# A hybrid encoder step on one core: scores from stacked float32r halves, attention groups in the order B, C, B, C, A, C, A, A

## The chip, the cores and the metric

The kernel runs on one core of a Trainium2 chip. The metric is the device time in microseconds of one execution; lower is less time. Engines are named TensorE (PE in the rows; PEld is its weight load), VectorE (DVE), ScalarE (ACT), GpSimd (POOL) and SyncE (SP), which issues all transfers of this kernel.

## The reference

Two layers are applied to a prompt of 1024 tokens and to 8 samples of 16 new tokens with 256 past tokens each (1152 token rows in all, in 9 tiles of 128; tile 8 is the samples). Everything is float32. For each layer:

```
h = rms_norm(x, norm_mix);  qa,ka,va,qb,kb,vb,qc,kc,vc,fz = split(h @ w_in)      # q and k of each head normed
A: 6 q heads, 2 k/v heads, 64 wide: softmax(q k/8 + bias, window of own and 2 previous chunks of 64, a sink in the sum) v
B: 4 heads, two maps of 32: softmax(q0 k0 ..) - lam * softmax(q1 k1 ..), times v, then a norm    # bias, all earlier chunks
C: 6 heads, 64 wide: softmax(q k/8 + cum_q - cum_k, causal) v                     # cum: running sum of log forget gates
x = x + concat(A, B, C) @ w_out
x = x + (silu(h2 @ w_gate) * (h2 @ w_up)) @ w_down,  h2 = rms_norm(x, norm_ffn)
```

The caches of keys, values and gates are outputs too.

## The kernel before, in words

`build` runs `setup` once and then, in a loop over the layers, `project`, `attend`, `mix` and `feed`. Each of them is a phase: it has its own buffers and semaphores, and the engines meet at its end. x stays in SBUF for the whole run.

`setup` (lines 149 to 232) loads x, turns the bias table into rows of 10 heads (stored at L180), and loads them back skewed: tiles with 16 rows outermost (L187, L188), and the samples' pieces with 8 batches outermost (L193, L194).

`project` computes h @ w_in in 6 blocks of columns times 9 tiles. Each product is three passes of float32r (high x high, high x low, low x high: L410 to L412); `split_hi` (ScalarE, L238) and `split_lo` (VectorE, L243) make the halves. Raw weights pass through a ring of 4. VectorE reads the result out into `nat`, norms the heads, SyncE stores it to the scratch tensor `qkv` and to the caches (L539), TensorE transposes q and k back to back with later units, ScalarE takes them out into `tT` (a ring of 4), and SyncE stores them as float32 to the scratch `qkT` (1792 rows of 1152 tokens, L512).

`attend` goes through 8 groups, each of two heads (four maps in B), in the order written at line 806: A, A, A, B, B, C, C, C. A group has 18 units: 2 heads times 9 tiles of 128 queries. Each engine runs the same loop over iterations u in program order. TensorE: `score(u)` (plain float32 products of q with the keys, 128 to 1024 columns in pieces of 512, L988; the samples at L995 and L997), `turn(u - 2)` (transposes of p, L1013), extra transposes of past keys (L1027) or of finished outputs (L1035), `values(u - 3)` (L1050, L1059). VectorE: `front(u)` adds the bias row and takes the maximum in one instruction (L1175), then makes the bias of the exponential (L1179 to L1186); `back(u - 1)` makes the reciprocal and, in B, combines the two maps (L1204); `take_out` scales the output, one instruction a unit (L1225). ScalarE: the exponential with its row sum (L1091), the copies of the transposed p (L1105). In A and C, q of a head lies in the upper or lower 64 of 128 partitions with zeros elsewhere (GpSimd clears them, L958, L964), so one product with all 128 rows of kT gives one head; B does so with 32 rows.

SyncE's program sets when a group's data come. `load_front(g)` waits until group g - 2 has been scored (two buffers), loads kT (L888), the bias or gate rows (L891 to L901) and qT (L904) on one semaphore, which `score` waits for at the group's first unit, then v (L907). `load_past(g)` loads past keys (L920), past values (L927), which wait until all values of group g - 1 are multiplied, and the samples' queries `qpast` (L935), which wait for GpSimd's clear (L962) after group g - 1's last score. The order is

```
load_front(groups[0]); ...constants...; load_past(groups[0]); load_front(groups[1])
for g in groups:
    load_past(groups[g.index + 1])
    load_front(groups[g.index + 2])
    sp.wait_ge(evacuated, place["mix", g.index, 2] + 1); sp.dma_start(t["mixT"]..., mixTb[:])     # L952
```

`mix` multiplies the stored outputs by w_out in three float32r passes and adds to x (L1334); `feed` is the FFN (L1526 adds to x), with loops over 22 blocks of D_FF, and stores y (L1408).

Of the kernel before, what the change touches and what calls it, by code (L numbers as in the profile page):

```python
# [19 lines left out]
P = 128  # L20
D_MODEL, SEQ, DEPTH, DEC_BATCH, DEC_SEQ, PAST = 1024, 1024, 2, 8, 16, 256
CHUNK, HEAD = 64, 64
# [4 lines left out]
EPS, NEG = 1e-6, -1e30  # L27
TP = SEQ // P
T = TP + 1
# [15 lines left out]
GAINS = [("q_norm_a", 0, 6, HEAD, HEAD ** -0.5), ("k_norm_a", 384, 2, HEAD, None),  # L45
         ("q_norm_b", 512, 8, B_DIM, B_DIM ** -0.5), ("k_norm_b", 768, 8, B_DIM, None),
         ("q_norm_c", 1024, 6, HEAD, HEAD ** -0.5), ("k_norm_c", 1408, 6, HEAD, None)]
GAIN_AT = [0, 512, 768, 1024, 1408]

# [12 lines left out]
def constants():  # L62
# [16 lines left out]
        "c_causal": np.where(i[None, :] <= i[:, None], 0.0, NEG).astype(np.float32),  # L79
        "c_batch": np.where(same, 0.0, NEG).astype(np.float32),  # L80
        "c_batch_causal": np.where(same & (i[None, :] <= i[:, None]), 0.0, NEG).astype(np.float32),
# [20 lines left out]
class Phase:  # L102
# [16 lines left out]
    def close(self):  # L119
        with self.nc.Block() as block:  # L120
            @block.gpsimd
            def _(pool):
                numbers = sorted(s.num for s in self.sems)
                assert numbers == list(range(numbers[0], numbers[-1] + 1))
                pool.sem_clear(range(numbers[0], numbers[-1] + 1))
        self.ctx.close()
# [6 lines left out]

def build(nc, t):

    with ExitStack() as ctx:
        def sb(name, shape, dt=F32):
            return ctx.enter_context(nc.sbuf_tensor(name, shape, dt))

        k = {"x": sb("x", [P, T, D_MODEL]), "ident": sb("ident", [P, P]),  # L140
             "ms": sb("ms", [P, T]), "logf": sb("logf", [P, T, C_HEADS]), "cumq": sb("cumq", [P, T, C_HEADS]),
             "lam": sb("lam", [P, 1])}
        setup(nc, t, k)
        with nc.Fori(0, DEPTH) as layer:
            project(nc, t, k, layer)
            attend(nc, t, k, layer)
            mix(nc, t, k, layer)
            feed(nc, t, k, layer)


def setup(nc, t, k):
# [19 lines left out]
    with nc.Block() as block:  # L171
# [46 lines left out]
        def _(dve):  # L218
            dve.wait_ge(loaded, 48)
            dve.wait_ge(product, 1)  # L220
            dve.tensor_copy(row[:], pr[:, 0:REL]).then_inc(copied, 1)
            dve.wait_ge(tiles_in, 16 * (2 * P // COPIES + 2 * heads))

            dve.memset(tile_a[0:64, :, 192:256], NEG).then_inc(tiles_done, 1)
            dve.memset(tile_a[64:128, :, 0:64], NEG).then_inc(tiles_done, 1)
            dve.memset(tile_b[0:64, :, SEQ - 64:SEQ], NEG).then_inc(tiles_done, 1)
# [73 lines left out]
class GateSums:  # L300
# [7 lines left out]
    def __init__(self, nc, ph, t, k, layer, xn, h32, pt):  # L308
# [18 lines left out]
        self.lam_s, self.lam_e = rows_[:, at:at + 2], rows_[:, at + 2:at + 4]  # L327
        self.prow, self.srow = pt[:, 0, :], pt[:, 1, 0:PAST]
        self.cols, self.nrow = pt[:, 1, 512:512 + T * C_HEADS], pt[:, 1, PAST:PAST + P]
        self.loaded, self.past_sum, self.col_sums, self.totals, self.sums, self.negated, self.stored = (  # L330
            ph.sem(n) for n in ("gate_loaded", "past_sum", "col_sums", "totals", "sums", "negated", "cum_stored"))
# [3 lines left out]
    def load(self, sp):  # L335
# [10 lines left out]
        sp.dma_start(self.lam_c, t["c_lam"][0:1, bass.ds(layer, 1)].broadcast_to([P, 1])).then_inc(self.loaded, 16)  # L346

    def store(self, sp):
        sp.wait_ge(self.negated, 3)
# [32 lines left out]
    def dve_totals(self, dve):  # L382

        dve.wait_ge(self.past_sum, 1)
        dve.tensor_scalar(self.past_row, self.srow[0:self.BH, :], -1.0, None, ALU.mult).then_inc(self.negated, 1)
        dve.tensor_scalar(self.total, self.is_batch, self.srow[0:self.BH, PAST - 1:PAST], None, ALU.mult).then_inc(self.totals, 1)
        dve.wait_ge(self.col_sums, 1)
        dve.tensor_copy(self.k["cumq"][:, 0:TP, :], self.cols[:, 0:TP * C_HEADS].rearrange("p (t h) -> p t h", t=TP)).then_inc(self.totals, 1)

    def pe_totals(self, pe):  # L390

        new, cols = self.k["logf"][:, TP, :], self.cols[:, TP * C_HEADS:T * C_HEADS]
# [1222 lines left out]
```

## Time and profile before

| | us |
|---|---|
| median of 3 runs | 3482.25 (3479.91 to 3482.97) |
| profiled execution, its own time | 3486.92 |
| its span, first to last instruction | 3485.3 |
| TensorE busy | 3209.2 (92%) |
| weight loads busy | 2875.4 (83%) |
| VectorE busy | 1688.8 (48%) |
| ScalarE busy | 1076.2 (31%) |
| GpSimd busy | 354.5 (10%) |
| DMA: moved, mean share of 16 engines | 274.95 MB, 28% |

Layer 1 runs: setup and start to 78 us, projection to 408, attention to 828, output projection to 941, FFN to 1769; layer 2 repeats it, with its attention from 2108 to 2528. A share is busy time over the stretch; "granted clock" is the part of TensorE's full 2.4 GHz that it was given. The DMA share is the mean over 16 engines, so one engine busy alone shows as 0.06. Every DMA in this kernel goes through SyncE's queue, and an entry of that queue's timeline is the time to issue, not to move.

### The profile page before, as it was taken

Reading aid. Unit: us, or ns where it says so; the run is one execution under the profiler, and the core shown is the slowest. Engines: PE = TensorE matmul, PEld = TensorE weight load, DVE = VectorE, ACT = ScalarE, POOL = GpSimd, SP = SyncE. Lnnn points to the kernel's source line nnn. Section 1 sums busy time; section 2 is a strip of 40 time slices with the busy share of each in tenths; the row PEclk is TensorE's granted clock in tenths of the full one; section 3 lists DMA queues with packets and bytes.
Section 4 is the critical chain, followed back from the end, with each engine's and each line's share of the span. In section 5 each row is a group of like instructions: output and inputs, shape, how many; then the busy total and the mean of one; then the engine's idle time right before and its main releaser. Section 6 shows DMA issues by size and latency. Waiting matters only on the chain. (4 is left out here: it accounts for less than half of the span.)

```text
span 3485.3 us, 50528 instructions
## 1 busy us (share of the span) xinstructions
PE 3209.2 (92%) x18146; PEld 2875.4 (83%) x18146; DVE 1688.8 (48%) x4058; ACT 1076.2 (31%) x2321; POOL 354.5 (10%) x216
## 2 busy tenths in 40 slices
PE   0699899998899999999968997999988999999999
PEld 0589777786799999999957896777778999999998
DVE  0344378644245445445445445784433454454454
ACT  1332266554231111111123225665524111111112
POOL 0222010000010100100012211010001001001000
PEclk9899899998999999999989998999999999999999
DMA  7244554333021111111024445525132111111111
GB/s 175 79 138 137 158 122 107 88 83 117 19 67 37 54 36 36 54 36 36 24 90 127 135 137 139 132 70 131 35 103 67 37 36 54 36 38 52 36 36 61
DMA packets 368395, 274.95 MB, mean 79 GB/s; under 512 B 128546, under 2 KB 336366, under 8 KB 368186
## 3 DMA queue, kind: packets, MB, share of 16 engines
q1 hardware_dynamic: 368218, 272.70, 28.0%
q8 instruction: 98, 1.61, 0.2%
q14 instruction: 79, 0.65, 0.1%
HBM read 195.84 MB, written 78.62 MB: 79 GB/s over the span
## 5 line engine op out<-in xcount | busy, mean ns | idle before, releaser
L1526 DVE TENSOR_TENSOR x<-x,ffn_down 128x512 f32<-128x512 f32 x792 | 509.5, 684 | 0.0
L1548 DVE TENSOR_TENSOR ffn_xn<-ffn_xn,ffn_up 128x384 f32<-128x384 f32 x132 | 73.2, 554 | 752.7 <-ACT ffn_xn L1493 752.7
L410 PE MATMUL ffn_up<-ffn_h_hi,ffn_hi_g 128*128 128x384 f32 x1056 | 355.4, 337 | 2.0 <-DVE ffn_h_lo L243 2.0
L410 PE MATMUL ffn_up<-ffn_h_hi,ffn_hi_u 128*128 128x384 f32 x1056 | 355.2, 336 | 0.0
L412 PE MATMUL ffn_up<-ffn_h_hi,ffn_lo_g 128*128 128x384 f32 x1056 | 354.8, 336 | 0.0
L412 PE MATMUL ffn_up<-ffn_h_hi,ffn_lo_u 128*128 128x384 f32 x1056 | 354.8, 336 | 0.0
L411 PE MATMUL ffn_up<-ffn_h_lo,ffn_hi_g 128*128 128x384 f32 x1056 | 354.8, 336 | 0.0
L411 PE MATMUL ffn_up<-ffn_h_lo,ffn_hi_u 128*128 128x384 f32 x1056 | 354.8, 336 | 0.0
L988 PE MATMUL att_S<-att_kT,att_qT 128*128 128x512 f32 (+3 forms) x864 | 324.1, 491 | 32.7 <-DMA att_qT<-scratch_qkT 25.7
L1493 ACT ACTIVATE ffn_xn<-ffn_up 128x384 f32<-128x384 f32 x132 | 64.9, 492 | 858.5 <-PE ffn_up L412 858.5
L410 PE MATMUL prj_acc<-prj_w_hi,prj_h_hi 128*128 128x384 f32 (+2 forms) x864 | 318.1, 368 | 0.0
L411 PE MATMUL prj_acc<-prj_w_lo,prj_h_hi 128*128 128x384 f32 (+2 forms) x864 | 309.3, 358 | 0.0
L412 PE MATMUL prj_acc<-prj_w_hi,prj_h_lo 128*128 128x384 f32 (+2 forms) x864 | 309.0, 358 | 0.0
L410 PE MATMUL ffn_down<-ffn_hi_d,ffn_a_hi 128*128 128x512 f32 x792 | 308.2, 389 | 0.0
L411 PE MATMUL ffn_down<-ffn_lo_d,ffn_a_hi 128*128 128x512 f32 x792 | 308.1, 389 | 0.0
L412 PE MATMUL ffn_down<-ffn_hi_d,ffn_a_lo 128*128 128x512 f32 x792 | 308.1, 389 | 0.0
L1175 DVE CUSTOM_DVE_ANT_0 att_s<-att_S,att_add_p 128x256 f32<-128x256 f32 (+7 forms) x320 | 208.5, 651 | 132.0 <-PE att_S L991 82.3
L1091 ACT ACTIVATE att_p<-att_s,att_bias 128x128 f32<-128x128 f32 (+3 forms) x360 | 242.3, 675 | 57.7 <-DVE att_bias L1179 30.3
L1416 POOL TENSOR_TENSOR ffn_raw_g<-ffn_raw_g,ffn_gain 128x1024 f32<-128x1024 f32 x44 | 83.5, 1898 | 1629.5 <-DMA ffn_raw_g<-in_w_gate 1629.5
L988 PEld LDWEIGHTS att_S<-att_kT,att_qT 128*128 128x128 f32 x864 | 146.0, 197 | 105.1 <-issue 62.4
L1050 PE MATMUL att_O<-att_vn,att_pT 128*128 128x64 f32 x1800 | 231.6, 269 | 0.0
L1105 ACT ACTIVATE att_pT<-att_TR 128x256 f32<-128x256 f32 (+3 forms) x368 | 157.3, 450 | 235.8 <-PE att_TR L1013 235.7
(174 smaller groups left out, 5749.6 us busy)
## 6 DMA issues: line engine op xcount, KB each, us to landing
ffn_raw_g<-in_w_gate SPq DMA_DIRECT2D x44, 512.0 KB, 4.0
ffn_raw_u<-in_w_up SPq DMA_DIRECT2D x44, 512.0 KB, 5.1
ffn_raw_d<-in_w_down SPq DMA_DIRECT2D x44, 512.0 KB, 5.0
scratch_qkv<-prj_nat SPq DMA_DIRECT2D x72, 192.0 KB, 1.9
prj_w_raw<-in_w_in SPq DMA_DIRECT2D x64, 192.0 KB, 2.5
scratch_qkv<-prj_nat SPq DMA_DIRECT2D x36, 256.0 KB, 2.1
att_kT<-scratch_qkT SPq DMA_DIRECT2D x16, 576.0 KB
att_vn<-scratch_qkv SPq DMA_DIRECT2D x16, 576.0 KB, 8.3
```

Source lines behind the costliest of these rows:

```text
L410: pe.matmul(out, l_hi, r_hi, start=first, stop=False)
L411: pe.matmul(out, l_hi, r_lo, start=False, stop=False)
L412: return pe.matmul(out, l_lo, r_hi, start=False, stop=final)
L988: last = pe.matmul(out[:, c:c + w], q, kT[:, b, k0 + c:k0 + c + w], start=True, stop=not (g.kind == "C" and c + w == n))
L1050: last = pe.matmul(O[:, u % 2, 0:HEAD], pT[:, u % 2, x * P:(x + 1) * P], vn[:, b, kt, v], start=(x == 0), stop=(x == len(ks) - 1))
L1091: act.activation(p[:, u % 3, r, 0:n], s[:, job % 2, 0:n], ACT.Exp, bias=bias[:, job:job + 1], accum_out=total[:, job:job + 1]).then_inc(ex ...
L1105: act.activation(pT[:, u % 2, c * 512:c * 512 + w], TR[:, n % 2, 0:w], ACT.Copy).then_inc(evacuated, 1)
L1175: dve.tensor_tensor_reduce(s[:, job % 2, 0:n], S[:, job % 2, 0:n], extra_row, 1.0, -3e38, ALU.add, ALU.max, mx[:, one]).then_inc(biased, 1)
L1416: pool.tensor_tensor(raw[n][:], raw[n][:], gain[:].unsqueeze(2).broadcast_to([P, KD, P]), ALU.mult).then_inc(scaled[n], 1)
L1493: act.activation(sg[:, b, :], up[:, b, 0, 0:384], ACT.Silu).then_inc(activated, 1)
L1526: dve.tensor_tensor(x, x, down[:, (q * ND + n) % 4, :], ALU.add).then_inc(added, 1)
L1548: dve.tensor_tensor(a32[:, b, :], sg[:, b, :], up[:, b, 1, 0:384], ALU.mult).then_inc(gated, 1)
```

## The change

In `project`, q and k are no longer stored as float32. ScalarE and VectorE split each transposed block into high and low float32r parts, both are stored to a scratch `qk_parts` (2, 1792, 1152), and only v goes to a scratch `v` (1152, 768) in place of `qkv`. The samples' q are also stored in float32 (`q_own`). The ring of raw weights falls from 4 to 3, that of transposed blocks from 4 to 2. x gives up its SBUF space in the attention and is loaded again in `mix`.

In `attend`, a score product runs on stacks in float32r: in A and C the q stack is (high, low) on 128 partitions, and there are two key stacks, (high, high) and (low, low), so two products; in B the q stack is (high, high, low, low) and the key stack (high, low, high, low), so one. The signs are turned, so that the minimum of bias - score is the exponential's bias directly, without further instructions; p is written in place in a ring of 6. A column of ones beside v gives A and C their row sums, so v has 65 columns. Outputs are taken out four tiles at a time. SyncE issues the constants of the attention ahead of load_front(groups[0]) now. The layer loop is written out. The core of the diff:

```diff
+SCRATCH_MORE = {"v": (TOK, N_V), "qk_parts": (2, N_QK, TOK), "q_own": (N_QK, P)}
@@ project
-    RAW, RING = 4, 12
+    RAW, RING = 3, 12
-    tT = ph.sb("tT", [P, 4, 512])
+    tT_hi, tT_lo = ph.sb("tT_hi", [P, 2, 512], F32R), ph.sb("tT_lo", [P, 2, 512], F32R)
-                sp.dma_start(dst, tT[:, m % 4, 0:n * P].rearrange("p (x n) -> p x n", n=P)).then_inc(qk_stored[m % 4], 16)
+                for half, part in enumerate((tT_hi, tT_lo)):
+                    dst = t["qk_parts"][half, GAIN_AT[b]:GAIN_AT[b] + n * P, i * P:(i + 1) * P].rearrange("(x p) n -> p x n", p=P)
+                    sp.dma_start(dst, part[:, m % 2, 0:n * P].bitcast(F32).rearrange("p (x n) -> p x n", n=P)).then_inc(qk_stored[m % 2], 16)
+            def cut_turned(m):
+                split_lo(dve, tT_lo[:, m % 2, 0:n], turn[:, m % 2, 0:n], tT_hi[:, m % 2, 0:n]).then_inc(cut_qk, 1)
@@ attend
-        [("A", 0), ("A", 1), ("A", 2), ("B", 0), ("B", 1), ("C", 0), ("C", 1), ("C", 2)])]
+        [("B", 0), ("C", 0), ("B", 1), ("C", 1), ("A", 0), ("C", 2), ("A", 1), ("A", 2)])]
+    qs, ks = ph.sb("qs", [P, 2, 4, TOK], F32R), ph.sb("ks", [P, 2, 4, TOK], F32R)
@@ load_front
-                sp.dma_start(kT[:, b, :], t["qkT"][g.k_row:g.k_row + P, :]).then_inc(sem, 16)
+                low_part = N_QK * TOK
+                for m in range(g.maps):
+                    q, key = g.q_row(m) * TOK, (g.k_row + m * g.D) * TOK
+                    if kind == "B":
+                        for half in range(2):
+                            own = slice(half * 2 * B_DIM, (half + 1) * 2 * B_DIM)
+                            sp.dma_start(qs[own, b, m, :].bitcast(F32), rows(t["qk_parts"], q + half * low_part, [[0, 2], [TOK, B_DIM], [1, TOK]])).then_inc(sem, 16)
+                            sp.dma_start(ks[own, b, m, :].bitcast(F32), rows(t["qk_parts"], key, [[low_part, 2], [TOK, B_DIM], [1, TOK]])).then_inc(sem, 16)
+                    else:
+                        sp.dma_start(qs[:, b, m, :].bitcast(F32), rows(t["qk_parts"], q, [[low_part, 2], [TOK, HEAD], [1, TOK]])).then_inc(sem, 16)
+                        for half in range(2):
+                            sp.dma_start(ks[:, b, 2 * m + half, :].bitcast(F32), rows(t["qk_parts"], key + half * low_part, [[0, 2], [TOK, HEAD], [1, TOK]])).then_inc(sem, 16)
...
-                for m in range(g.maps):
-                    sp.dma_start(qT[m * g.D:(m + 1) * g.D, b, m, :], t["qkT"][g.q_row(m):g.q_row(m) + g.D, :]).then_inc(sem, 16)
-                sp.dma_start(vn[:, b, :, :], qkv[:, :, g.v_col:g.v_col + P]).then_inc(v_in[b], 16)
+                for h in range(2):
+                    sp.dma_start(vn[:, b, :, h, 0:HEAD], v[:, :, g.v_col + h * HEAD:g.v_col + (h + 1) * HEAD]).then_inc(v_in[b], 16)
@@ score
-                            last = pe.matmul(out[:, c:c + w], q, kT[:, b, k0 + c:k0 + c + w], start=True,
+                            for x in stacks:
+                                last = pe.matmul(out[:, c:c + w], q, ks[:, b, x, k0 + c:k0 + c + w], start=x == stacks[0],
@@ front
-                    dve.tensor_tensor_reduce(s[:, job % 2, 0:n], S[:, job % 2, 0:n], extra_row, 1.0, -3e38, ALU.add, ALU.max, mx[:, one]).then_inc(biased, 1)
...
+                    dve.tensor_tensor_reduce(p[:, job % RING, 0:n], S[:, job % 2, 0:n], extra_row, 1.0, ceiling,
+                                             ALU.add, ALU.min, low[:, job:job + 1]).then_inc(biased, 1)
@@ exps
-                    act.activation(p[:, u % 3, r, 0:n], s[:, job % 2, 0:n], ACT.Exp, bias=bias[:, job:job + 1],
-                                   accum_out=total[:, job:job + 1]).then_inc(exped, 1)
+                        act.activation(p[:, job % RING, 0:n], p[:, job % RING, 0:n], ACT.Exp, bias=low[:, one], scale=-1.0).then_inc(exped, 1)
@@ mix
+            sp.dma_start(k["x"][:, 0:TP, :], x_rows[0].rearrange("a (t p) d -> p (a t) d", p=P)).then_inc(x_in, 16)
+            sp.dma_start(k["x"][:, TP, :], x_rows[1].rearrange("b s d -> (b s) d")).then_inc(x_in, 16)
```

## Rows read from the trace of the kernel before

**Rows 1.** Windows of two stages: stretch, busy time of PE, PEld, DVE, ACT, POOL; clock, DMA, GB/s
```profile
78.00:408.00 330.00, 284.47 (x1530) 259.65 (x1530) 135.07 (x337) 93.38 (x210) 67.20 (x49) 0.95 0.39 120
408.00:828.00 420.00, 387.92 (x2680) 312.69 (x2680) 263.59 (x1046) 248.40 (x671) 27.01 (x14) 0.95 0.42 101
```

**Rows 2.** Groups of instructions of TensorE in the first layer's attention
```profile
L988 PE MATMUL att_S<-att_kT,att_qT 128*128 128x512 f32 (+3 forms) x432 | 162.2, 492 | 16.3 <-DMA att_qT<-scratch_qkT 12.9 <-DVE att_mx L1175 3.4
...
L1050 PE MATMUL att_O<-att_vn,att_pT 128*128 128x64 f32 x900 | 115.8, 269 | 0.0
```

**Rows 3.** Timeline of TensorE in a unit of group B: start, us, instructions
```profile
583.13 1.98 PE L988 MATMUL att_S<-att_kT,att_qT 128*128 128x512 f32 x4
584.95 0.38 PE L1013 MATMUL att_TR<-ident,att_p 128*128 128x128 f32 x2
```

**Rows 4.** Timeline of TensorE in the FFN, nine intervals apart
```profile
2715.72 0.39 PE L410 MATMUL ffn_down<-ffn_hi_d,ffn_a_hi 128*128 128x512 f32 x1
...
2717.76 0.39 PE L410 MATMUL ffn_down<-ffn_hi_d,ffn_a_hi 128*128 128x512 f32 x1
```

**Rows 5.** Windows of three stretches of the setup, columns as in rows 1
```profile
9.00:11.00 2.00, 0.00 (x0) 0.00 (x0) 1.14 (x1) 0.00 (x0) 0.00 (x0) 1.00 1.03 424
18.00:20.00 2.00, 0.00 (x0) 0.00 (x0) 0.00 (x0) 0.00 (x0) 0.00 (x0) 1.00 0.55 78
54.00:56.00 2.00, 0.00 (x0) 0.00 (x0) 0.00 (x0) 0.00 (x0) 0.00 (x0) 1.00 0.55 122
```

**Rows 6.** Timeline of SyncE's queue in the setup: start, us to issue
```profile
10.16 0.97 SPq L180 DMA_DIRECT2D scratch_bias_rows<-set_row  x1
...
55.67 0.57 SPq L193 DMA_DIRECT2D set_samp_b<-scratch_bias_rows  x1
```

**Rows 7.** DMA issues, whole run: count, KB each, us to landing where told
```profile
att_qT<-scratch_qkT SPq DMA_DIRECT2D x24, 288.0 KB
...
att_kp<-in_cache_c_k SPq DMA_DIRECT2D x24, 256.0 KB, 4.6
...
att_add_s<-scratch_cum_past SPq DMA_DIRECT2D x12, 128.0 KB
```

**Rows 8.** Timeline of GpSimd: the qpast clear, as each group's last score is done
```profile
443.58 0.95 POOL L962 MEMSET att_qpast<- 128x1024 f32 x1 [30.75 <-PE att_S L997]
...
469.53 0.95 POOL L962 MEMSET att_qpast<- 128x1024 f32 x1 [25.00 <-PE att_S L997]
...
571.11 0.95 POOL L962 MEMSET att_qpast<- 128x1024 f32 x1 [63.83 <-PE att_S L997]
...
643.27 0.95 POOL L962 MEMSET att_qpast<- 128x1024 f32 x1 [67.33 <-PE att_S L997]
...
702.17 0.95 POOL L962 MEMSET att_qpast<- 128x1024 f32 x1 [54.07 <-PE att_S L997]
...
757.15 0.95 POOL L962 MEMSET att_qpast<- 128x1024 f32 x1 [54.02 <-PE att_S L997]
```

**Rows 9.** Timeline of SyncE's queue in the first layer's attention
```profile
407.97 0.32 SPq L888 DMA_DIRECT2D att_kT<-scratch_qkT  x1
...
449.18 0.37 SPq L927 DMA_DIRECT2D att_vp<-in_cache_a_v  x1
...
583.23 1.00 SPq L927 DMA_DIRECT2D att_vp<-in_cache_b_v  x2
...
584.28 8.75 SPq L935 DMA_DIRECT2D att_qpast<-scratch_qkT  x16
...
655.50 3.22 SPq L935 DMA_DIRECT2D att_qpast<-scratch_qkT  x4
...
828.09 0.32 SPq L1289 DMA_DIRECT2D mix_m_raw<-scratch_mixT  x1
```

**Rows 10.** Groups of VectorE by shape, both layers: count, busy us, mean ns
```profile
L1175 DVE CUSTOM_DVE_ANT_0 att_s<-att_S,att_add_p 128x1024 f32<-128x1024 f32 x28 | 34.3, 1223 | 17.7 <-PE att_S L991 14.2 <-PE att_S L988 3.5
...
L1204 DVE SCALAR_TENSOR_TENSOR att_p<-att_p,att_coef 128x1024 f32<-128x1024 f32 x8 | 10.3, 1286 | 0.3
```

More of the change, by code:

```diff
@@ L123, in _ @@
                 numbers = sorted(s.num for s in self.sems)
-                assert numbers == list(range(numbers[0], numbers[-1] + 1))
-                pool.sem_clear(range(numbers[0], numbers[-1] + 1))
+                first = numbers[0]
+                for a, b in zip(numbers, numbers[1:] + [None]):
+                    if b != a + 1:
+                        pool.sem_clear(range(first, a + 1))
+                        first = b
         self.ctx.close()
@@ L425, in stores @@
         flat = f"({shape})"
+        if first in V_AT:
+            out.append((t["v"][i * P:(i + 1) * P, V_AT[first]:V_AT[first] + count], src))
         if sample:
@@ L486, in project @@
     order = [sum(bool(NORMED[v[0]]) for v in work[:u]) for u in range(NW)]
+    b_order = [sum(bool(x) for x in NORMED[:b]) for b in range(len(IN_BLOCKS))]
     def splits_at(u):
@@ L551, in _ @@
                     gates.store(sp)
-            for m in range(4):
-                sp.wait_ge(qk_stored[m], 16 * len(range(m, len(normed_units), 4)))
+            for m in range(2):
+                sp.wait_ge(qk_stored[m], 32 * len(range(m, len(normed_units), 2)))
+            sp.wait_ge(own_stored, 16 * sum(bool(x) for x in NORMED))
             for u in range(NW - 4, NW):
@@ L821, in attend @@
     NJ = jobs_to[-1]
-    mx, bias, total, inv, esink = (ph.sb(n, [P, NJ]) for n in ("mx", "bias", "total", "inv", "esink"))
+    unit_of = [u for u in range(NU) for _ in range(units[u][0].per_head)]
+    low, total, inv, esink, den = (ph.sb(n, [P, NJ]) for n in ("low", "total", "inv", "esink", "den"))
     coef = ph.sb("coef", [P, NU])
-    sink = ph.sb("sink", [P, A_HEADS])
+    sink, far_sink = ph.sb("sink", [P, A_HEADS]), ph.sb("far_sink", [P, A_HEADS])
     mask_f, mask_s = ph.sb("mask_f", [P, P]), ph.sb("mask_s", [P, P])
@@ L859, in attend @@
     weighed_to = [sum(x[0].kind == "B" for x in units[:u]) for u in range(NU + 1)]
-    sinks_to = [sum(x[0].kind == "A" for x in units[:u]) for u in range(NU + 1)]
-    n_qk = {"A": 2 + 1 + 4, "B": 4 + 1 + 4, "C": 2 + 1 + 6}
-    def fresh(g):
-        return g.index < 2 or "B" in (g.kind, groups[g.index - 2].kind)
+    parts_to = [sum(x[2] in (HALF - 1, TP - 1, TP) for x in units[:u]) for u in range(NU + 1)]
+    sunk_to = [sum(x[0].kind == "A" and x[2] in (HALF - 1, TP - 1, TP) for x in units[:u]) for u in range(NU + 1)]
+    n_qk = {"A": 4 + 4 + 2, "B": 16 + 4, "C": 4 + 6 + 2}
     def to(g, parity, count):
@@ L875, in chunk_of_mix, with ends_part, part_of, first_jobs @@
         return c * 4, min(c * 4 + 4, T)
+    def ends_part(u):
+        return units[u][2] in (HALF - 1, TP - 1, TP)
+    def part_of(u):
+        i = units[u][2]
+        return [u] if i == TP else list(range(u - i % HALF, u - i % HALF + HALF))
+    def first_jobs(u):
+        us = part_of(u)
+        step = units[u][0].per_head
+        return slice(jobs_to[us[0]], jobs_to[us[-1]] + 1, step)
     with nc.Block() as block:
@@ L956, in _ @@
         def _(pool):
-            for b in range(2):
-                pool.memset(qT[:, b, 0:2, :], 0.0).then_inc(q_zeroed[b], 1)
+            pool.memset(vn[:], 1.0).then_inc(ones_set, 1)
             for g in groups:
@@ L996, in score @@
                                       start=(c == 0), stop=(c == g.nb - 1))
-                        last = pe.matmul(out[:, g.n_past:g.n_samp], q, kT[:, b, SEQ:TOK], start=True, stop=True)
+                        for x in stacks:
+                            last = pe.matmul(out[:, g.n_past:g.n_samp], q, ks[:, b, x, SEQ:TOK], start=x == stacks[0], stop=x == stacks[-1])
                     last.then_inc(scored, 1)
@@ L1208, in back @@
[L1208 to L1218 removed]
+                then(dve.reciprocal(inv[:, a + 1:e], total[:, a + 1:e]))
```

314 lines of the change are left out of this document (172 added, 142 removed).

## The prediction

> **What bounds the kernel now.** I read the stage windows first. In the first layer's attention (408 to 828 us) TensorE is busy 387.92 of 420 us, while VectorE has 263.59 and ScalarE 248.40, and the DMA engines stand at a share of 0.42 [rows 1]. The projection before it is TensorE's too, with VectorE at 135.07 of 330 us [rows 1]. Then the groups of instructions of the attention: the float32 score product is TensorE's dearest, 162.2 us, and only 16.3 us of idle time stand before it, most of it one wait for the first q load of the layer [rows 2]. So attention is bound by TensorE's instruction stream, and its loads are hidden but for the first. That is what the change wants to use, and it is true only as long as the loads stay hidden; the rest of the argument is about them.
>
> **Scores, the part that gets cheaper.** Two float32 products of 512 columns take 1.82 us from start to next start [rows 3], 1.78 ns a column. A float32r product of 512 columns takes 2.04/9 = 0.227 us [rows 4], 0.443 ns a column. A layer scores 11,520 columns in A, 36,864 in B and 27,648 in C: 76,032 x 1.78 = 135 us now. After: A and C need two stacked products, B one: (2 x 39,168 + 36,864) x 0.443 = 51 us. TensorE is relieved of 84 us a layer. Widths of 128 and 256 columns have no float32r row here; between the float32 price and the line above they move the sum by under 15 us a layer.
>
> **The stack loads, the part that gets dearer.** Before, a group loads kT once and qT in two or four pieces, 1.1 MB, each transfer with one row of 4.6 KB for each partition (1152 float32), and all of it with 64 or 128 rows as the outermost dimension. After, q and k come as high and low parts, doubled: a B group issues 16 transfers of 64 rows of 4,608 B, an A or C group 6 of 128 rows. The source of each is written with an outermost dimension of 2, ([0, 2] or [low_part, 2]), ahead of 32 or 64 rows. What does an outermost dimension do? Three rows answer. The load of x, outermost 128, moves 424 GB/s at a share of 1.03 [rows 5]: all 16 engines, 25.7 GB/s each. The store of the bias rows has an outermost dimension of 10 (heads) and is issued at 10.16 us, behind x; when x is in, the share is 0.55 [rows 5, 6], under 10/16. The samples' bias loads, outermost 8 in the source though 128 partitions are written, run at 0.55, issued one behind another 0.6 us apart [rows 5, 6], near or under 8/16. And the group of loads that holds such a source (cum_past, 8 x 16 rows) shows no landing time at all, nor do q loads on the same semaphore, where the C keys, outermost 128, show 4.6 us [rows 7]: not all its parts report as 16 would. I take it that a transfer is spread over as many engines as its outermost dimensions on both sides allow, so two here, and that the two are always the same ones, since back-to-back loads of outermost 8 never got near a share of 1.
>
> One of these rows then costs 4,608/25.7 = 0.179 us on its engine. A B group has 16 x 64/2 = 512 rows on each of two engines, 91.7 us; an A or C group 6 x 128/2 = 384 rows, 68.7 us. Behind them in the same queues, and under the same wait, come the bias or gate rows (1.4 MB in B and C, 3.5 us on all engines; 0.5 MB in A, 1.3 us), and some 2 us to land: 97 us for B, 74 for C, 72 for A. Against that the groups compute in 72 us (B), 55 (C) and 26 (A) today [rows 8]. So every group's load is longer than the compute it should hide behind, even at the old compute times. What the faster scores save is then hidden in the wait for the next load.
>
> The Trainium skill, page "DMA: Bandwidth & Descriptors", section "Why a DMA increments its semaphore by 16 and not by 1", states the rule as such: the largest number up to 16 that divides both sides' slowest dimension, and from the hardware queues always the lowest-numbered engines. By that rule the sum is the same as by the rows, two fixed engines, and the trace agrees with its shares of 0.55 for 10 and 8. It speaks against this change, and it is not needed for any number here.
>
> **When a load can start.** SyncE works in order: for group g+1 it issues load_past(g+1), whose v part waits until all values of group g are multiplied, which TensorE reaches only some units into group g+1; then the qpast pieces; only then load_front(g+2). In the trace the v load comes 5.6 us after the group's last score where A follows A, and 12.1 where B follows B [rows 8, 9]. Then 1 us for it, then 3.2 us of qpast issues in C (8.75 in B) [rows 9]; I take C's for A. So loads don't overlap: each begins after the group before it has begun. I take a start lag of 11 us where B or C meet, 8 where A meets C.
>
> From the first issue (t = 0), in the new order B, C, B, C, A, C, A, A: constants 3 us, first B load 97: scores start at 100 us. Group 1 (C): its load is already queued behind 11 us of B's past keys and values: +85. Then lag + v + qpast + load: group 2 (B) 11+1+3.3+97 = 112; group 3 (C) 11+1+9+74 = 95; group 4 (A) 11+1+3.3+72 = 87; group 5 (C) 8+1+3+74 = 86; group 6 (A) 8+1+3.3+72 = 84; group 7 (A) 8+1+3+72 = 84. Last: today the last group, a C, runs 70.9 us from its start to the first load of the output projection [rows 8, 9]; an A is 29 us shorter: 42. Sum 100+85+112+95+87+86+84+84+42 = 775 us, where it is 420.1 now (407.97 to 828.09) [rows 9]. **+355 us a layer, +710 for two.**
>
> **The rest.** The order of the groups costs or gains almost nothing of this: the sum of the loads is the same in any order; B first exposes 97 rather than 72 us. The bias, reciprocal and take-out instructions removed from VectorE and the accumulator reads removed from ScalarE lie beside TensorE and now beside waits: 0. The values product grows from 64 to 65 columns: at most 1/64 of 115.8 us [rows 2], 2 us a layer, under the waits: 0. The v load falls into 256 B pieces in two transfers over all engines, behind the scores' wait: 0. In the projection VectorE gets 45 more cuts of about 0.6 us, 25 us beside 135 of 330 [rows 1]: hidden, 0; SyncE has one more store a unit, and the raw-weight ring falls from 4 to 3, so one load at a block's end comes late: 0 to 3 us at each of 5 borders, I take 1: 10 for two layers. The reload of x (4.6 MB, 12 us at 25.7 GB/s an engine) is issued behind the last weights of the output projection, while TensorE still multiplies: 0, at most 5 a layer; without that cover 12. The cleared clock: waits of tens of us let the granted clock fall, but a group computing at half speed (A: 52, B: 144, C: 110) would pass the next load's time in B and C, and it is back up within the group: 0 taken, in the range.
>
> Sum: the profiled execution took 3486.9 us for a span of 3485.3, and the median of the three runs is 3482.3. 3487 + 710 + 10 = 4207, less 2 us for the sample scores: **4205 us**. A measurement here can tell 0.2% from no change.
>
> **Rivals.**
> *The loads spread over all engines after all* (the compiler or the queue splits rows otherwise). For it: nothing in rows 5 has an outermost 2, and the rule is read from 8 and 10. Against it: those shares. Then 4.7 MB takes 12 us, all hides as before, and the 84 us a layer come through, less what VectorE holds back in B: a unit of 1024 columns needs two reductions of 1223 ns and a combination of 1286 ns [rows 10], 3.7 us plus small ones, against about 3.5 of TensorE, some 9 us a layer. 3487 - 2 x 75 + 16 (longer first load) + 10 = **3363**. It decides from the point where a load and its lag are shorter than the group's compute, 26 us in A, so from seven or eight engines on. Chance 0.10.
> *Two engines, but another pair for each transfer.* The 16 transfers of 5.7 us then run side by side; price as above plus one transfer's latency of 11 us at the starts: **3400**. Chance 0.03.
> *Two engines at a lower rate.* Over the attention the engines moved 101 GB/s at 0.42, 15.0 GB/s each, because of short rows [rows 1]. With stack rows crowded down to that end, 593 us of stacks a layer become 1015 and the kernel 5050; to 20 GB/s, 4550. The stack rows are as long as those of x, so 25.7 is the near row. Chance of over 4450: 0.05.
> *The load order overlaps better than I read it.* Lags and issues of 85 us a layer vanish: 4035. In my range.
>
> **How the numbers follow.** Two fixed engines near 25.7 GB/s: 0.81, forecast 4205, with 4035 and 4450 as its ends. That holds its 8 in 10 alone, so the range isn't stretched to the fast cases. Faster 0.13 (rivals one and two), slower 0.86, within 0.2% 0.01 (a partial spread that just cancels).
>
> **What would show it.** Right: in the changed profile, scores preceded by long idle time that q or k stack loads end, seven times a layer at 70 to 100 us distance; a DMA share near 2/16 within those waits, about 0.3 over the attention; float32r 512-column scores at 0.227 us; attention near 775 us a layer; FFN unchanged. Wrong: scores waiting on VectorE or nothing, and attention under 400 us. A start lag or rate that is off would show in the distances between the groups' qpast clears alone.

## The result, and the profile after

The changed kernel takes 4347.64 us, the median of 4 runs (4337.68 to 4353.49), against 3482.22 us (3479.91 to 3482.97) in the same session: a ratio of 1.2484, 95% interval 1.246 to 1.2508. The profiled execution took 4348.24 us for a span of 4346.5.

The first lines of the page say what kind of loss this is:

```profile
PE 3187.1 (73%) x17930; PEld 2928.3 (67%) x17930; DVE 1579.4 (36%) x3264; ACT 1046.4 (24%) x2067; POOL 319.7 (7%) x206
...
PE   2798053574369999999969944445344899999999
...
PEclk9899576766679999999989976777566999999999
DMA  6344222222241111111024422222232411111111
```

The row of PE has two holes, one in each layer, at slices 5 to 12 and 24 to 31 (of 40, counted from 1); the granted clock sinks in them and the DMA row holds at 2 in most of them. The second half of each layer is at 9, as before. The windows of the first layer give the sizes: projection, attention, two stretches inside waits of the attention, and the FFN (columns as in rows 1):

```profile
78.00:427.40 349.40, 294.99 (x1526) 266.88 (x1526) 151.48 (x381) 94.88 (x214) 66.42 (x49) 0.93 0.39 115
427.40:1261.20 833.80, 376.42 (x2576) 341.59 (x2576) 192.76 (x605) 231.59 (x539) 9.59 (x9) 0.66 0.26 76
440.00:500.00 60.00, 0.00 (x0) 0.00 (x0) 0.00 (x0) 0.00 (x0) 0.00 (x0) 0.50 0.13 52
1170.00:1200.00 30.00, 0.00 (x0) 0.00 (x0) 0.00 (x0) 0.00 (x0) 0.00 (x0) 0.50 0.14 56
1373.00:2202.00 829.00, 820.17 (x4385) 774.90 (x4386) 400.72 (x590) 153.27 (x222) 83.42 (x44) 0.99 0.14 42
```

Attention takes 833.8 us where it took 420 [rows 1], the projection 349.4 where it took 330. No compute engine does anything in the two stretches, while the DMA engines stand at 0.13 and 0.14, about two of sixteen, and move 52 and 56 GB/s, 26 to 28 for each of the two. The FFN takes as long as before (829 us). What ends TensorE's waits is in the waits view of the attention (total us, times, longest):

```profile
PE att_S L1061 <- DMA att_add_s<-scratch_bias_sb: 174.5, 2, 109.4
PE att_S L1061 <- DMA att_add_s<-scratch_cum_new: 142.1, 3, 58.3
PE att_S L1061 <- DMA att_add_s<-scratch_bias_sa: 115.9, 3, 54.2
```

Two B groups, three C groups and three A groups: every one of the eight waits, 432.5 us together, where the only such wait before was one of 12.9 us [rows 2]. The transfer named is a small one. It stands last in the group's queue, under the semaphore that the stacks count on too; the large ones ahead of it show in SyncE's own timeline (start, us to issue):

```profile
430.30 0.53 SPq L958 DMA_DIRECT2D att_ks<-scratch_qk_parts  x1
...
436.61 6.09 SPq L957 DMA_DIRECT2D att_qs<-scratch_qk_parts  x1
442.75 5.43 SPq L958 DMA_DIRECT2D att_ks<-scratch_qk_parts  x1
...
498.90 5.43 SPq L958 DMA_DIRECT2D att_ks<-scratch_qk_parts  x1
504.37 5.40 SPq L968 DMA_DIRECT2D att_add_p<-scratch_bias_b  x1
```

After the first few, most issues of a stack in a B group take 5.43 us instead of 0.5, and those of the A and C groups, twice as large, 11.1: SyncE itself is held back at the pace at which two engines empty the queue. From start to start it is 5.47 us for 32 rows on each, a little less than the 32 x 0.179 = 5.7 us of the forecast's price. The starts of the groups stand in TensorE's timeline, here groups 3 to 8 of layer one:

```profile
747.56 0.69 PE L1061 MATMUL att_S<-att_ks,att_qs 128*128 128x128 f32 x2 [65.12 <-DMA att_add_s<-scratch_bias_sb]
...
854.26 0.69 PE L1061 MATMUL att_S<-att_ks,att_qs 128*128 128x128 f32 x2 [43.42 <-DMA att_add_s<-scratch_cum_new]
...
942.73 0.69 PE L1061 MATMUL att_S<-att_ks,att_qs 128*128 128x128 f32 x2 [25.98 <-DMA att_add_s<-scratch_bias_sa]
...
1038.77 0.69 PE L1061 MATMUL att_S<-att_ks,att_qs 128*128 128x128 f32 x2 [58.27 <-DMA att_add_s<-scratch_cum_new]
...
1127.98 0.69 PE L1061 MATMUL att_S<-att_ks,att_qs 128*128 128x128 f32 x2 [35.72 <-DMA att_add_s<-scratch_bias_sa]
...
1219.54 0.69 PE L1061 MATMUL att_S<-att_ks,att_qs 128*128 128x128 f32 x2 [54.22 <-DMA att_add_s<-scratch_bias_sa]
```

An A group, 26 us of compute before [rows 8], now keeps its place for 92 us (1127.98 to 1219.54), like a C group (854.26 to 942.73).

### The profile page after: what moved, and what is told of

The parts are those of the page before. It is cut to its first block and busy times, and to the rows that moved or that the text cites. A ratio compares the mean times of both kernels' runs of the same rounds, so it can differ in the third digit from the quotient of the medians.

```text
span 4346.5 us, 47890 instructions
## 1 busy us (share of the span) xinstructions
PE 3187.1 (73%) x17930; PEld 2928.3 (67%) x17930; DVE 1579.4 (36%) x3264; ACT 1046.4 (24%) x2067; POOL 319.7 (7%) x206
## 5 line engine op out<-in xcount | busy, mean ns | idle before, releaser
L1061 PE MATMUL att_S<-att_ks,att_qs 128*128 128x512 f32 (+3 forms) x672 | 205.6, 408 | 879.0 <-DMA att_add_s<-scratch_bias_sb 348.5
L1061 PEld LDWEIGHTS att_S<-att_ks,att_qs 128*128 128x128 f32 x672 | 126.1, 226 | 898.6 <-DMA att_add_s<-scratch_bias_sb 349.4
L1256 DVE CUSTOM_DVE_ANT_0 att_p<-att_S,att_add_p 128x128 f32<-128x128 f32 (+3 forms) x224 | 164.4, 756 | 557.5 <-PE att_S L1061 245.3
L1124 PE MATMUL att_O<-att_vn,att_pT 128*128 128x65 f32 x1800 | 273.4, 301 | 0.0
L1124 PEld LDWEIGHTS att_O<-att_vn,att_pT 128*128 128x128 f32 x1800 | 268.3, 226 | 0.7 <-ACT att_pT L1181 0.5
L1493 POOL TENSOR_TENSOR ffn_raw_g<-ffn_raw_g,ffn_gain 128x1024 f32<-128x1024 f32 x44 | 83.5, 1898 | 1674.0 <-DMA ffn_raw_g<-in_w_gate 1674.0
```

Source lines behind the costliest of these rows:

```text
L1061: last = pe.matmul(out[:, c:c + w], q, ks[:, b, x, k0 + c:k0 + c + w], start=x == stacks[0], stop=x == stacks[-1] and not (masked and c + ...
L1124: last = pe.matmul(O[:, bank, at:at + VW], pT[:, u % 2, x * P:(x + 1) * P], vn[:, b, kt, h, :], start=(x == 0), stop=(x == len(tiles) - 1))
L1256: dve.tensor_tensor_reduce(p[:, job % RING, 0:n], S[:, job % 2, 0:n], extra_row, 1.0, ceiling, ALU.add, ALU.min, low[:, job:job + 1]).then ...
L1493: pool.tensor_tensor(raw[n][:], raw[n][:], gain[:].unsqueeze(2).broadcast_to([P, KD, P]), ALU.mult).then_inc(scaled[n], 1)
```

## The experiments

The theory: the outermost size 2 in the source of each stack load puts the transfer on two engines, always the same two; that alone costs the time. Rivals: the number of issues and the doubled bytes are too much for the queue; the order of the groups; the smaller ring of raw weights; or something in the float32r rewrite itself.

### The two slowest sizes exchanged

Same bytes to the same places, same count of transfers, one edit in four sources:

```diff
-rows(t["qk_parts"], q + half * low_part, [[0, 2], [TOK, B_DIM], [1, TOK]])
+rows(t["qk_parts"], q + half * low_part, [[TOK, B_DIM], [0, 2], [1, TOK]])
-rows(t["qk_parts"], key, [[low_part, 2], [TOK, B_DIM], [1, TOK]])
+rows(t["qk_parts"], key, [[TOK, B_DIM], [low_part, 2], [1, TOK]])
-rows(t["qk_parts"], q, [[low_part, 2], [TOK, HEAD], [1, TOK]])
+rows(t["qk_parts"], q, [[TOK, HEAD], [low_part, 2], [1, TOK]])
-rows(t["qk_parts"], key + half * low_part, [[0, 2], [TOK, HEAD], [1, TOK]])
+rows(t["qk_parts"], key + half * low_part, [[TOK, HEAD], [0, 2], [1, TOK]])
```

As the destination is left as it was, its rows are filled in another order, (row, part) instead of (part, row), alike in q and k stacks; each product still sums high and low parts over all dimensions.

> The changed kernel with the first two dimensions of the source of every stack load exchanged: 32 or 64 rows outermost, then the 2 of high and low (or of the repeat). Same bytes, same number of transfers, same rows of 4,608 B; only the order of partitions within a stack changes, alike for q and k. Theory (the outermost dimension sets how many DMA engines take part, and the two are always the same): loads hide again, attention near 360 us a layer in place of 834, time about 3390 us (3350 to 3430). Rival (the doubled bytes or the number of issues on SyncE make the loads long): unchanged, 4347. Rival (the two engines rotate from transfer to transfer, and something else holds the loads): little changes, over 4200.

Measured: 3470.33 us (3462.55 to 3478.83), ratio to the kernel before 0.9968 [0.9953, 0.9983]. 877 us of the changed kernel's time are gone. The mechanism of the theory stands, the size of what is left does not: 80 us more than was expected, and above the expected range. Windows of its projection, its attention and a stretch inside the first wait:

```profile
78.00:426.50 348.50, 292.91 (x1526) 264.94 (x1526) 151.58 (x381) 95.18 (x214) 66.52 (x48) 0.93 0.40 115
426.50:816.00 389.50, 322.20 (x2576) 289.80 (x2576) 192.25 (x605) 232.07 (x539) 9.60 (x9) 0.90 0.63 164
430.00:455.00 25.00, 0.00 (x0) 0.00 (x0) 0.94 (x5) 0.00 (x0) 0.00 (x0) 0.50 1.02 242
```

The DMA share in the wait is 1.02 where it was 0.13. The rate didn't rise as much: 242 GB/s are 15 for each of 16 engines, where two engines moved 26 each and the load of x moved 25.7 each at the same share [rows 5]. Why the stack rows are slower when all engines fetch them, the runs don't show.

Attention takes 389.5 us, 30.5 less than before the change: TensorE's busy time fell by 65.7 us (387.92 to 322.20), and its idle time rose by 35. Where that went is in the waits of TensorE:

```profile
PE att_S L1061 <- DMA att_add_s<-scratch_bias_sb: 34.7, 1, 34.7
...
PE att_TR L1085 <- DVE att_p L1269: 10.1, 18, 1.0
PE att_TR L1107 <- ACT att_pT L1181: 5.6, 8, 1.9
PE att_TR L1099 <- DMA att_kp<-in_cache_b_k: 5.3, 1, 5.3
PE att_S L1061 <- DMA att_add_s<-scratch_cum_new: 3.3, 1, 3.3
PE att_TR L1099 <- DMA att_kp<-in_cache_c_k: 3.2, 1, 3.2
PE att_TR L1099 <- DMA att_kp<-in_cache_a_k: 2.5, 1, 2.5
```

The first wait of the layer is 34.7 us instead of 12.9, and past keys, which nothing waited for in the attention of the kernel before, come late by 11.0 us in all. At that rate the first group's 6.1 MB (stacks and bias rows) alone take 25 us.

### The same loads on four engines

Each load is split in two, and the source of each half gets 4 as its slowest size, with strides that don't run on into each other (one of the sources; the counts of the semaphore follow):

```diff
-sp.dma_start(qs[:, b, m, :].bitcast(F32), rows(t["qk_parts"], q, [[low_part, 2], [TOK, HEAD], [1, TOK]])).then_inc(sem, 16)
+for r in range(2):
+    own = slice(r * HEAD, (r + 1) * HEAD)
+    sp.dma_start(qs[own, b, m, :].bitcast(F32), rows(t["qk_parts"], q + r * low_part, [[TOK, 4], [4 * TOK, HEAD // 4], [1, TOK]])).then_inc(sem, 16)
-    n_qk = {"A": 4 + 4 + 2, "B": 16 + 4, "C": 4 + 6 + 2}
+    n_qk = {"A": 12 + 4, "B": 32 + 4, "C": 12 + 6}
```

> The change with each stack load split into halves whose sources have four as their slowest size, with strides that cannot be merged into one; the bytes on each half come out in another order. Theory: the engines that a transfer takes follow the slowest size, so that four share what two carried; the loads of each group take half as long, about 302 us per layer less of measured distances between group starts: 3743 us (3680 to 3800), with the DMA share in the waits near 4/16 where it was 2/16. Rival: the stack loads are slow for another reason (bytes, count of issues), then about 4347 us. This kernel permutes the order of the rows in a stack, so scores are not the reference's.

Measured: 3782.48 us (3776.97 to 3791.61), ratio 1.0855 [1.0836, 1.0874], inside the expectation's range. The rows are permuted alike in q and k, so the same terms are summed, against what the expectation says of the scores. A stretch inside the first wait, and TensorE's waits in the first attention:

```profile
437.00:455.00 18.00, 0.00 (x0) 0.00 (x0) 0.00 (x0) 0.00 (x0) 0.00 (x0) 0.50 0.26 105
```

```profile
PE att_S L1067 <- DMA att_add_s<-scratch_bias_sb: 67.6, 2, 61.8
PE att_S L1067 <- DMA att_add_s<-scratch_cum_new: 53.9, 3, 31.2
PE att_S L1067 <- DMA att_add_s<-scratch_bias_sa: 27.7, 2, 22.6
```

Twice the share, twice the GB/s. With 2, 4 and 16 engines the waits for a group's loads are 432.5, 149.2 and 38.0 us in the first layer, and the times 4348, 3782 and 3470. The time follows the slowest size of the source, step by step. Here the loads are twice as many and the bytes the same, so the count of issues isn't the price.

### The same defect put into the kernel before

```diff
-sp.dma_start(kT[:, b, :], t["qkT"][g.k_row:g.k_row + P, :]).then_inc(sem, 16)
+for m in range(P // g.D):
+    sp.dma_start(kT[m * g.D:(m + 1) * g.D, b, :], rows(t["qkT"], (g.k_row + m * g.D) * TOK, [[TOK, 2], [2 * TOK, g.D // 2], [1, TOK]])).then_inc(sem, 16)
-    t["qkT"][g.q_row(m):g.q_row(m) + g.D, :]).then_inc(sem, 16)
+    rows(t["qkT"], g.q_row(m) * TOK, [[TOK, 2], [2 * TOK, g.D // 2], [1, TOK]])).then_inc(sem, 16)
```

> The kernel before with the sources of the q and k head loads written with two as the slowest size, strides that cannot be merged: the same bytes, on two engines by the theory instead of all. Each group's loads then take about 23 us instead of 3, most of it beside 50 to 60 us of TensorE's work on a group, so the first group of each layer and the short ones pay: 3548 us (3520 to 3590). Rival: the shape of a source sets nothing, 3482 us. This kernel permutes the rows of the heads alike in q and k.

Measured: 3590.19 us (3588.63 to 3591.57), ratio 1.031 [1.0292, 1.0327]. The direction is right, the size at the very end of the range: +109 us over the kernel before, where +66 was expected. A stretch inside the first wait, and the wait for q loads in the first attention:

```profile
425.00:429.00 4.00, 0.00 (x0) 0.00 (x0) 0.00 (x0) 0.00 (x0) 0.00 (x0) 0.50 0.13 52
```

```profile
PE att_S L989 <- DMA att_qT<-scratch_qkT: 67.1, 4, 32.3
```

The share is 0.13 here too, at 52 GB/s. 12.9 us in one wait became 67.1 in four. With 1.1 MB a group the defect costs 3%; with stacks of 3.5 to 4.7 MB it costs 25%. It was no part of the float32r arithmetic.

### Two designs that tested nothing of what they were made for

Before these two, the same question was put with other strides, rows taken in halves or quarters that lie one behind the other:

```diff
-[[0, 2], [TOK, B_DIM], [1, TOK]]
+[[B_DIM // 4 * TOK, 4], [TOK, B_DIM // 4], [1, TOK]]
```

in the changed kernel, with each load split in two; and in the kernel before

```diff
-t["qkT"][g.k_row:g.k_row + P, :]
+rows(t["qkT"], g.k_row * TOK, [[P // 2 * TOK, 2], [TOK, P // 2], [1, TOK]])
```

> The changed kernel with each stack load split into its two halves and each half's source written with an outermost dimension of 4: four engines if the theory holds, twice as many transfers of half the size. Theory: the stack rows take half their time, 46 us less in B and 34 less in A and C, no load shorter than its group's compute by much: some 296 us a layer, time 3755 (3700 to 3850). Rival (issues or bytes): at or over 4347.

Measured: 3491.77 us (3488.47 to 3511.8), ratio 1.0032 [1.0017, 1.0047].

> The kernel before, with the sources of kT and qT written with an outermost dimension of 2 (same bytes, same rows, same partitions). Theory: a group's 1.1 MB takes 23 us in place of 3; the first load is 20 us longer, and the loads issued behind an A group (26 us of compute, 9 of lag and issues) come some 9 and 4 us late, the others stay hidden: +33 us a layer, 3548 (3520 to 3580). Rival (bytes or issues): 3482.

Measured: 3483.16 us, ratio 0.9998 [0.9988, 1.0007].

Both missed. The first one's window inside the first wait shows why:

```profile
432.00:455.00 23.00, 0.00 (x0) 0.00 (x0) 0.94 (x5) 0.00 (x0) 0.00 (x0) 0.50 1.03 224
```

All engines, not four. An outer step that is exactly the inner size times the inner step describes one run of evenly spaced rows, and both runs fit with its being handled as one. So the size that counts is not the one written, but that left when such neighbours are joined; where they are joined, in the program's making or on the chip, the runs don't show. What the first run does tell: twice as many loads on all engines cost 3492 against 3470 us, 0.6%, which bounds the price of the issues alone. The second, by this reading, is the same transfers twice.

### The order of the groups

The changed kernel with the old order, then the exchanged sources with the old order:

```diff
-        [("B", 0), ("C", 0), ("B", 1), ("C", 1), ("A", 0), ("C", 2), ("A", 1), ("A", 2)])]
+        [("A", 0), ("A", 1), ("A", 2), ("B", 0), ("B", 1), ("C", 0), ("C", 1), ("C", 2)])]
```

> The changed kernel with the groups in the order A, A, A, B, B, C, C, C. If the order costs or gains nothing because the sum of the loads is the same: the first load is A's (some 35 us less exposed a layer), the last group is a C (some 30 us more), so 4347 within 1%. If the interleaving was worth anything under these loads: over 4390.

Measured: 4374.96 us (4367.96 to 4383.35), ratio to the kernel before 1.2549 [1.2528, 1.257], 0.6% above the changed kernel and within the 1% that was expected.

> The swapped stack loads with the groups in the order A, A, A, B, B, C, C, C. With the sources swapped TensorE waited 34.7 us for the first group, which is B; the kernel before, which starts with A, waited 12.9 us. Theory: that first wait is about all that the order moves, some 17 to 20 us per layer given back, and little lost elsewhere: 3435 us (3425 to 3460). Rival: the order hides the large transfers of B behind TensorE's work of C, and without it two B groups in a row wait: no gain or a loss, 3470 to 3500 us.

Measured: 3454.03 us (3451.88 to 3458.08), ratio 0.992 [0.9903, 0.9936], against 0.9968 [0.9953, 0.9983] in the new order: inside the expected range, though 19 us above its middle value. The waits that begin its groups:

```profile
PE att_S L1061 <- DMA att_add_s<-scratch_bias_sa: 21.3, 1, 21.3
...
PE att_S L1061 <- DMA att_add_s<-scratch_bias_sb: 9.9, 1, 9.9
```

The first wait falls from 34.7 to 21.3 us, and 9.9 us come back where B follows the short A groups. In the profiled executions the attention is 3 us shorter in the first layer (386.5 against 389.5) and 10 in the second (383.3 against 393.6); where those 10 come from isn't resolved. The sign of the order depends on the loads: with two engines the new order is 27 us better, with all of them 16 us worse. Either way it is small beside the 865 us of the change.

### The ring of raw weights

Cut to three in the kernel before, alone; and set back to four in the kernel with exchanged sources, where the space is found by placing one tile in another that is idle then:

```diff
-    RAW, RING = 4, 12
+    RAW, RING = 3, 12
```

```diff
-    RAW, RING = 3, 12
+    RAW, RING = 4, 12
-    tT_own = ph.sb("tT_own", [P, 512])
+    tT_own = xn[:, 1, 0:512]
```

> The kernel before with the projection's ring of raw weight blocks cut from four buffers to three, nothing else. Theory: the ring alone costs the projection what it costs in the changed kernel; giving it back there took 42 us off, so here up to 40 us are added: 3520 us (3505 to 3530). Rival: in the kernel before it is hidden, and something else of the change was late with it: 3482 us.

Measured: 3524.0 us (3513.83 to 3533.52), ratio 1.0104 [1.0088, 1.012].

> The swapped stack loads with the projection's ring of raw weight blocks back at four buffers (the space is found in a tile that is idle then). Theory: the projection's 18.5 us per layer above the kernel before, seen in both kernels with the changed ring, come from the three-deep ring: up to 37 us of 3470 go, 3433 us (3430 to 3445). Rival: they come from something else of the change, 3470 us.

Measured: 3428.21 us (3424.11 to 3438.94), ratio 0.9839 [0.9823, 0.9856].

+40 us in one kernel, inside its range, -42 in the other, 2 us beyond its range. First the window of the projection of the kernel before with three buffers, then that of the exchanged sources with four:

```profile
78.00:427.80 349.80, 294.40 (x1530) 266.58 (x1530) 134.73 (x337) 92.97 (x210) 66.71 (x49) 0.94 0.37 113
```

```profile
78.00:407.10 329.10, 284.37 (x1526) 259.52 (x1526) 151.97 (x380) 94.46 (x214) 66.28 (x48) 0.95 0.42 122
```

Both windows end where SyncE issues the attention's first load, as those above do. 349.8 us with three and the old arithmetic (330 with four [rows 1]), 329.1 with four and the new (348.5 with three): the additional cuts of VectorE (152 against 135 us busy) cost nothing, the ring alone costs 19 to 20 us a layer, and that twice is all of the 40 and 42 us. What TensorE waits for is in the waits of the projection of the kernel before with three buffers; neither line stands there with four:

```profile
PE prj_turn L577 <- DVE prj_nat L725: 6.0, 5, 1.9
...
PE prj_acc L410 <- DVE prj_w_lo L243: 3.0, 4, 0.9
```

Nine waits of 9.0 us together are about half of the 19.8 us; the other half is busy time of TensorE, 294.4 against 284.5 us for the same 1530 instructions, at a granted clock of 0.94 against 0.95. In the profiled execution of the kernel with exchanged sources and four buffers, which was the slowest of its four, the first attention gave 13 us back (402.3 against 389.5, clock 0.87 against 0.90), the second none (394.0 against 393.6); why the clock stood lower in the first is open.

### All three together

Exchanged sources, a ring of four, the old order.

> The swapped stack loads, the raw weight ring at four buffers, and the groups in the order A, A, A, B, B, C, C, C. Theory: the two savings are in different stages and add up: 3470 less 16 for the order and 42 for the ring, 3412 us (3400 to 3425). Rival: the projection's end, now earlier, exposes the first loads of the attention again and half of the order's gain goes: 3420 us.

Measured: 3414.26 us (3408.43 to 3415.21, 5 runs), ratio to the kernel before 0.9794 [0.9781, 0.9808]: it beats both kernels, the changed one by 933 us. The two savings add up (3470 - 16 - 42 = 3412), as was expected; the rival's 3420 lies above all five runs. Its projection and attention:

```profile
78.00:407.40 329.40, 284.47 (x1526) 259.21 (x1526) 152.10 (x381) 94.99 (x214) 66.21 (x49) 0.96 0.42 122
407.40:793.10 385.70, 325.80 (x2576) 292.67 (x2576) 192.14 (x605) 232.19 (x539) 9.57 (x9) 0.90 0.62 165
```

## Why the prediction was right, and where its sizes were off

The forecast was 4205 us, the time 4348: of 865 us added, 723 were forecast. Its likeliest case happened by its own mechanism: two engines, always the same, for every stack load. The missing 143 us aren't scatter between runs; they lie in terms that were sized too low. Point by point.

**Two engines at 25.7 GB/s each: right.** From outermost sizes of 8 and 10 [rows 5] the forecast went down to 2. Its rows fitted only roughly: the share of 0.55 for size 8, which it called near or under 8/16, is above it. The waits show a share of 0.13 and 52 to 56 GB/s. By the rule of the Trainium skill ("DMA: Bandwidth & Descriptors", section "Why a DMA increments its semaphore by 16 and not by 1") it would be two of the lowest-numbered engines; the trace agrees in the number, and in that many transfers waiting together stayed at 0.13 to 0.14, which also speaks against another pair for each transfer. Rival two (3400) and rival three (a lower rate, over 4450) fell on the same rows. (By the forecast's own prices the stacks are 2 x 91.7 + 6 x 68.7 = 596 us a layer, not the 593 in rival three.)

**The loads, 97, 74 and 72 us: right, a little low.** From the first stack's issue to the first score it takes 101.5 us in the third group (B: 646.04 in SyncE's timeline to 747.56 in TensorE's), and 73 to 78 in the A and C groups behind it. Over the six loads of groups 3 to 8 that makes some 16 us a layer more than forecast. The stack rows aren't the cause: 16 transfers at 5.47 us are 87.5 us where 91.7 were priced, six at 11.1 are 66.6 where 68.7 were. The excess is in what stands before and behind them in the queues, which the forecast put at 3 to 6 us; it isn't split further.

**The start lag, 11 and 8 us: the term that was mis-sized.** The load of past values, behind which the next stacks queue, was issued 15.6 us after the third group's first score, 15.4 after the fifth's:

```profile
763.14 0.99 SPq L1001 DMA_DIRECT2D att_vp<-in_cache_b_v  x2
```

Over six groups the lags are 83.5 us where 57 were forecast, +27 a layer. The step that failed is "the cleared clock: 0 taken". It held that a group at half speed would still pass under the next load. But the next load doesn't start until TensorE has done the first units of the group, and it does these right after a long wait, at the low clock. Windows of the lag of the second, third and fifth group:

```profile
627.00:642.00 15.00, 14.89 (x91) 13.98 (x91) 3.22 (x13) 4.01 (x9) 0.00 (x0) 0.57 0.34 74
747.50:763.00 15.50, 15.44 (x86) 15.01 (x86) 4.28 (x20) 5.49 (x17) 0.00 (x0) 0.50 0.61 108
942.70:958.00 15.30, 15.27 (x87) 14.90 (x87) 1.87 (x8) 3.64 (x8) 0.00 (x0) 0.50 0.32 78
```

TensorE is busy throughout, at a granted 0.50 to 0.57, the lower of its two levels for most of the time. The kernel with exchanged sources does the same work in these stretches, and mostly without a wait before it. From the third group's first score to SyncE's issue of its past values, and the same for the sixth group, which had to wait for its load:

```profile
562.04:570.39 8.35, 8.35 (x89) 8.11 (x88) 4.28 (x20) 5.58 (x19) 0.00 (x0) 1.00 0.42 55
696.93:708.38 11.45, 8.29 (x45) 7.26 (x45) 2.45 (x11) 2.84 (x7) 0.00 (x0) 0.50 0.70 151
```

At a granted 1.00 the third group's lag is 8.35 us, at 0.50 it was 15.6. The sixth group's stands at 0.50 in both kernels, and it takes 11.45 us in one and 11.6 in the other, 3.2 and 3.3 of them a wait for past keys. All six lags are 55.0 us with exchanged sources and 83.5 without, so the low clock costs 28.5 us a layer. That is the whole of the 27; the lags of 11 and 8 by themselves were even 2 us too long in sum.

**The first two starts, 100 and +85: 4 and 10 us more.** The second group's stacks were issued 18.4 us after the first score (531.72 to 550.07), not 11, because SyncE's issues of v, past keys, past values and qpast ahead of them took 34 us; the load itself took 77.0 us, not 74. The sum of the three points, 16 + 27 + 15, is 58 of the 59 us by which a layer's attention exceeds 775.

**The projection, +5 a layer: 19.4.** "One load at a block's end comes late, 1 us at each border": the runs with the ring alone changed show 40 to 42 us for two layers, not 10. The forecast counted waits only. The waits are there, 9.0 us in the first layer of the kernel before with three buffers, nearly twice the 5 taken; the rest is that TensorE's instructions are busy 10 us longer, for which the forecast had no term. Why they are is not shown.

**Together:** 2 x 59 + 2 x 14 = 146 over the forecast's 4205: 4351, where 4348 was measured. One error is hidden in the sum: over the six loads the stack rows were priced 15 us a layer too dear, and what stands around them in the queues 31 too cheap.

**Order, FFN, output projection, reload of x, added work of VectorE: 0, and it was near 0.** The order is worth 27 us (0.6%), so not quite nothing; VectorE's cuts are hidden, as the four-buffer projection shows.

**Rival one, all engines, 3363 us: its price was too good by 100.** The exchange of two sizes made this case true: 3470, and 3462 for the profiled execution. TensorE's busy time fell by 65.7 us a layer, not 84. From start to next start in the timeline the scores take some 76 us where 51 were forecast, and took 142 where 135 were. The groups by shape in the exchanged kernel's first attention show the reason (count, busy us, mean ns, idle time before):

```profile
L1061 PE MATMUL att_S<-att_ks,att_qs 128*128 128x512 f32 x120 | 45.8, 461 | 0.8 <-DVE att_low L1256 0.4
...
L1061 PE MATMUL att_S<-att_ks,att_qs 128*128 128x256 f32 x124 | 31.9, 335 | 0.3 <-DVE att_low L1256 0.3
L1061 PE MATMUL att_S<-att_ks,att_qs 128*128 128x384 f32 x40 | 12.6, 381 | 0.3 <-DVE att_low L1256 0.3
L1061 PE MATMUL att_S<-att_ks,att_qs 128*128 128x128 f32 x52 | 11.4, 290 | 38.0 <-DMA att_add_s<-scratch_bias_sb 34.7 <-DMA att_add_s<-scratch_cum_new 3.3
```

The columns are those of the forecast, 115,200. But 216 of the 336 products have 384 or fewer, and a product isn't paid by the column alone: from 512 to 256 to 128 columns the recorded mean falls from 461 to 335 to 290 ns, not by half each time (the records overlap, so they are no intervals). From start to next start, at a granted 1.00 in its timeline, a product takes 0.13 us at 128 columns, 0.165 at 256, 0.215 at 384 and 0.285 at 512: at every width 0.05 to 0.07 us more than the forecast's price by the column, which was read from products that stand back to back. The forecast bounded what the narrow ones could add by 15 us; with the 512-column products it was 25, of which some 19 are this surcharge, and 7 came back on the float32 side. The first load then costs 22 us more a layer where 8 were taken, as it was priced at 25.7 GB/s an engine and ran at 15; the past keys' waits 11 where 0 was taken, and the ring 18.5 where 5 was. So 2 x (9 + 14 + 11 + 13.5) = 95 of the 99 us between 3363 and 3462, with 9 for what 65.7 falls short of the 75 taken.

## What to carry to other kernels

Look at the source pattern of a load before its bytes: a repeat or a high and low pair written as the slowest size (here 2) puts the transfer on two of sixteen engines, at 52 GB/s, and exchanging it with the size behind it brings in all of them, here at 242 GB/s, for nothing. The sign in a profile is a DMA share standing at a small multiple of 1/16 in waits in which nothing else runs, with a releaser that is only the last and smallest of its queue. And when waits grow, price the work that stands between the wait's end and the next load at the low clock (15.6 us instead of 8.4 here), and a buffer taken from a ring by an experiment of its own: here one of four buffers was worth 1.2%, more than the new order of the groups.

## What the runs showed of the hardware beyond what was expected

- Neighbouring sizes whose strides run on into each other count as one: a written outermost size of 2 or 4 over adjoining rows ran on all engines (share 1.03 for 4; for 2, 3483.16 us against 3484.18 for the untouched kernel), the same number over interleaved rows on four (share 0.26).
- A queue full of slow transfers holds the issuing engine: 5.43 us (64 rows) or 11.1 (128 rows) for an issue that otherwise takes 0.5 to 0.6, so everything behind it in SyncE's order, past keys and qpast pieces included, leaves late too.
- Eight times the engines didn't bring eight times the rate: the same rows moved at 52 GB/s on two engines, 105 on four and 224 to 242 on all, 26 GB/s an engine on two and four and about 15 on sixteen (B's stacks, inside the first wait).
- The float32r score products pay mostly at 512 columns: from 128 to 512 columns the recorded mean rises only from 290 to 461 ns, and the time from start to next start from 0.13 to 0.285 us.
- Work behind a long wait stands at the lower clock: the same stretch of instructions took 15.6 us at a granted 0.50 and 8.35 at 1.00.
